# Deferring two thirds of the adaLN weights, and modulating a transposed x feature by feature

## What is computed

```python
def adaln(c, w_ada, b_ada):                      # c: 9 conditioning vectors (1 prompt, 8 samples)
    mod = jax.nn.silu(c) @ w_ada + b_ada         # w_ada is 1024 x 6144
    return mod.reshape(c.shape[0], 6, 1, D_MODEL)

def rmsnorm(x, g):
    xf = x.astype(jnp.float32)
    y = xf * lax.rsqrt(jnp.mean(jnp.square(xf), axis=-1, keepdims=True) + RMS_EPS)
    return (y * g.astype(jnp.float32)).astype(x.dtype)

def modulate(x, g, shift, scale):
    return rmsnorm(x, g) * (1.0 + scale) + shift

# modulate(x, g_mix, mod[:, 0], mod[:, 1]) is multiplied by w_in (1024 x 2856). Everything else
# (GLA, sparse attention, w_out, mixture of experts) comes after; mod[:, 2:6] is used only from w_out on.
```

## Time and profile before

| | |
|---|---|
| time, median of 3 executions | 2257.75 us (2255.24 to 2261.09) |
| the profiled execution | 2257.95 us, its span 2256.0 us |
| the stage `project` | 0 to 313.76 us of the span |
| PE, DVE, ACT, POOL busy over the span | 1863.9, 1465.3, 1085.5, 401.4 us |

### The profile page before, as it was taken

The page is one execution under the profiler, slowest core; times in us unless marked ns, Lnnn a source line. Parts: engine busy times, 40 slices in busy tenths (PEclk is TensorE's granted clock), DMA queues, the critical chain, the costliest instruction groups (busy, mean ns, idle before and its releaser), DMA issues. The chain is left out here.

```text
span 2256.0 us, 26455 instructions
## 1 busy us (share of the span) xinstructions
PE 1863.9 (83%) x8759; PEld 1403.3 (62%) x8759; DVE 1465.3 (65%) x1326; ACT 1085.5 (48%) x1015; POOL 401.4 (18%) x289
## 2 busy tenths in 40 slices
PE   7559976678886557707999999999999999999981
PEld 0038855466665343405777878787877778787861
DVE  1062227724443324436899898989898998989883
ACT  4021122333331111314767777777767677777761
POOL 0000010021000214040222222322222222223110
PEclk9769987696987678958999999999999999999996
DMA  4822142223000326046999999999999999999973
GB/s 177 346 93 70 39 89 101 62 89 113 1 1 3 111 98 188 24 124 242 351 357 377 361 369 368 370 368 361 377 354 380 360 377 361 375 366 370 372 269 106
DMA packets 119979, 525.52 MB, mean 233 GB/s; under 512 B 33629, under 2 KB 55022, under 8 KB 69327
## 3 DMA queue, kind: packets, MB, share of 16 engines
q1 hardware_dynamic: 105824, 487.26, 57.3%
q0 software_dynamic: 14096, 37.51, 6.7%
HBM read 503.17 MB, written 33.00 MB: 238 GB/s over the span
## 5 line engine op out<-in xcount | busy, mean ns | idle before, releaser
L2014 PE MATMUL banks<-split 128*128 128x512 f32 x4608 | 1086.8, 394 | 20.0 <-DVE split L2159 20.0
L2014 PEld LDWEIGHTS banks<-split 128*128 128x128 f32 x4608 | 858.7, 189 | 224.9 <-DVE split L2159 42.0
L2159 DVE TENSOR_TENSOR split<-expert_buffers,split 128x2048 fp32r<-128x2048 f32 x384 | 856.6, 2286 | 104.0 <-ACT split L2092 104.0
L2092 ACT ACTIVATE split<-expert_buffers 128x2048 fp32r<-128x2048 f32 x384 | 724.0, 1911 | 194.5 <-PE banks L2014 148.1
L1954 POOL TENSOR_TENSOR expert_buffers<-expert_buffers 128x1 f32<-128x1 f32 x64 | 66.8, 1044 | 775.8 <-issue 422.4
L2021 PE MATMUL banks<-expert_buffers 128*128 128x128 f32 x512 | 68.3, 277 | 58.7 <-DMA expert_buffers<-h_rows,expert_buffers 58.7
L1973 POOL DMA_INDIRECT ffn_rows<-expert_buffers x32 | 108.5, 3392 | 5.1 <-issue 4.6
L2021 PEld LDWEIGHTS banks<-expert_buffers 128*128 128x128 f32 x512 | 67.8, 192 | 63.8 <-issue 58.7
L408 PE MATMUL banks<-w_in_high,hT_high 128*128 128x476 f32 (+1 forms) x240 | 92.0, 383 | 1.5 <-ACT hT_high L278 1.5
L2107 ACT ACTIVATE expert_buffers<-expert_buffers 128x1024 f32<-128x1024 f32 x32 | 33.9, 1060 | 122.7 <-DVE expert_buffers L2170 122.7
L408 PE MATMUL banks<-w_in_low,hT_high 128*128 128x476 f32 (+1 forms) x240 | 91.7, 382 | 0.0
(11 more groups left out here) (310 smaller groups left out, 1924.4 us busy)
## 6 DMA issues: line engine op xcount, KB each, us to landing
expert_buffers<-in_w_gate SPq DMA_DIRECT2D x128, 1024.0 KB, 5.8
expert_buffers<-in_w_up SPq DMA_DIRECT2D x128, 1024.0 KB, 7.7
expert_buffers<-in_w_down SPq DMA_DIRECT2D x128, 1024.0 KB, 10.8
arena<-in_w_ada SPq DMA_DIRECT2D x8, 3072.0 KB, 12.3
w_in_landing<-in_w_in SPq DMA_DIRECT2D x6, 1904.0 KB, 8.5
arena<-in_x_prompt SPq DMA_DIRECT2D x8, 512.0 KB, 18.4
arena<-in_cache_cmp POOLq DMA_DIRECT2D x32, 128.0 KB, 3.3
arena<-in_cache_cmp SPq DMA_DIRECT2D x32, 128.0 KB, 2.8
```

What stands on the lines that cost most here:

```text
L2014: last = pe.matmul(ps[:, bank + c, :], x[:, kt * P:(kt + 1) * P].bitcast(F32R), wt.bitcast(F32R), start=False, stop=(kt == KT - 1 and x is ...
L2092: act.activation(high[:, j % RING_Q].bitcast(F32R), v, ACT.Copy).then_inc(s_high, 1)
L2159: dve.tensor_tensor(rest[:, j % RING_Q].bitcast(F32R), v, high[:, j % RING_Q], ALU.subtract).then_inc(s_rest, 1)
```

## The change

x is loaded ahead of any of w_ada. Of w_ada only the columns of shift and scale (the first 2048 of 6144) are loaded at first, in four pieces of 2 MB with buffers of their own; the other 4096 columns follow as 16 pieces of 1 MB, in two buffers that lie over x, and PE handles each after a given step of the projection (`place_of`), from step 5 to step 27 of 30. The first three chunks of w_in have buffers of their own and are queued right behind. The bias is loaded into `mod` beforehand and DVE adds the matmuls' result to it; the second part of that is done after the last step, and then columns 2048 to 6143 of `mod` are stored.

x, scaled only by its reciprocal root mean square, is transposed while w_ada arrives. Shift and scale are turned into columns by matmuls of 9 rows with the identity (L380's spreading is gone), and the modulation acts on the transposed x: `full(kt)` on a block of 128 features and all tokens, then ACT's rounding and DVE's rest for that block. The first four steps of the projection run block by block over four tiles at once; each block waits for its own rest.

```diff
@@ sp @@
+            sp.dma_start(c9[0:1, :], io["c_prompt"]).then_inc(s_c, 16)
+            sp.dma_start(c9[1:9, :], io["c_sample"]).then_inc(s_c, 16)
+            sp.dma_start(core.consts, io["consts"][:, 0:N_CONST_A + N_CONST_B]).then_inc(s_const, 16)
+            for t, (t0, n) in enumerate(TILES):
+                src = io["x_prompt"][0, t0:t0 + n, :] if t < ST else io["x_sample"].rearrange("b t d -> (b t) d")
+                sp.dma_start(x[0:n, t, :], src).then_inc(s_x, 16)
+            for i in range(4):
+                sp.dma_start(early[i], w_ada[:, 2 * i:2 * i + 2, 0:2 * D]).then_inc(s_early[i], 16)
             for j in range(4):
+                sp.dma_start(mod[32 * j:32 * j + 9, :, :], io["b_ada"].rearrange("a (b j n) -> a b j n", b=3, j=4)[:, :, j, :]
+                             .to_broadcast([9, 3, 512])).then_inc(s_b, 16)
+            sp.dma_start(gT, io["g_mix"].rearrange("a (p k) -> (a p) k", k=KT)).then_inc(s_g, 16)
+            for c in range(3):
+                load_w_in(c)
+            load_late(0)
+            load_late(1)
+            for i in range(NT, STEPS):
+                if i % NT == 0 and i // NT + 2 < NCH:
+                    load_w_in(i // NT + 2)
+                if i in place_of and place_of[i] + 2 < LATE:
+                    load_late(place_of[i] + 2)
+            sp.wait_ge(s_modcp, 12)
+            for j in range(4):
+                sp.dma_start(core.mod_d.rearrange("s (b j n) -> s b j n", b=3, j=4)[:, 1:3, j, :],
+                             mod[32 * j:32 * j + 9, 1:3, :]).then_inc(s_modout, 16)
             sp.wait_ge(s_modout, 64)
@@ act @@
+            for t, (t0, n) in enumerate(TILES):
+                link(act.activation(junk[0:n, :], x[0:n, t, :], ACT.Square, accum_out=stat[0:n, t:t + 1]))
             act.wait_ge(s_const, 16)
+            link(act.activation(stat[:, NT:2 * NT], stat[:, 0:NT], ACT.Ln, scale=1.0 / D, bias=core.const("eps")))
+            act.activation(stat[:, NT:2 * NT], stat[:, NT:2 * NT], ACT.Exp, scale=-0.5).then_inc(s_rstd, 1)
+            for t, (t0, n) in enumerate(TILES):
+                act.wait_ge(s_xT, t + 1)
+                act.activation(hT[:, 0:4, t0:t0 + n], x_banks(t)[:, 0], ACT.Copy).then_inc(s_xTa, 1)
             act.wait_ge(s_mod, 1)
             round_weights(0)
+            for kt in range(KT):
+                act.wait_ge(s_full, kt + 1)
+                act.activation(hTh[:, kt, :].bitcast(F32R), hT[:, kt, :], ACT.Copy).then_inc(s_hh, 1)
@@ dve @@
+                dve.tensor_scalar(tmp[0:n, t % 2, :], x[0:n, t, :], stat[0:n, NT + t:NT + t + 1], None, ALU.mult
+                                  ).then_inc(s_xn, 1)
+                if t >= 1:
+                    columns(t - 1)
...
+            dve.wait_ge(s_b, 64)
+            take_mod(0, 1)
+            dve.wait_ge(s_modT, 1)
...
+            def full(kt):
+                s = hT[:, kt, SEQ:NTOK].rearrange("p (b t) -> p b t", t=TS)
+                dve.tensor_scalar(hT[:, kt, 0:SEQ], hT[:, kt, 0:SEQ], scaleT[:, kt, 0:1], shiftT[:, kt, 0:1], ALU.mult, ALU.add)
+                link(dve.tensor_tensor(s, s, bcast(scaleT[:, kt, 1:9], 2, TS), ALU.mult))
+                dve.tensor_tensor(s, s, bcast(shiftT[:, kt, 1:9], 2, TS), ALU.add).then_inc(s_full, 1)
+            def rest_of_rows(kt):
+                dve.wait_ge(s_hh, kt + 1)
+                dve.tensor_tensor(hTl[:, kt, :].bitcast(F32R), hT[:, kt, :], hTh[:, kt, :], ALU.subtract).then_inc(s_hl, 1)
+            full(0)
+            rest_of_weights(0)
+            for kt in range(KT):
+                if kt + 1 < KT:
+                    full(kt + 1)
+                rest_of_rows(kt)
             rest_of_weights(1)
...
+            dve.wait_ge(s_mod, 2)
+            for b in (1, 2):
+                for j in range(4):
+                    rows = slice(32 * j, 32 * j + 9)
+                    dve.tensor_tensor(mod[rows, b, :], mod[rows, b, :], ps[rows, ADA + b, :], ALU.add).then_inc(s_modcp, 1)
@@ pe @@
+            for kt in range(KT):
+                if kt % 2 == 0:
+                    pe.wait_ge(s_early[kt // 2], 16)
+                last = modulation(kt, 0, early[kt // 2][:, kt % 2, :])
+            last.then_inc(s_mod, 1)
+            for n in range(4):
+                pe.wait_ge(s_modcp, n + 1)
+                rows = slice(32 * n, 32 * n + 9)
+                mv = mod[rows, 0, :].rearrange("s (p k) -> s k p", k=KT)
                 for kt in range(KT):
+                    last = pe.matmul(ps[64 * (n % 2):64 * (n % 2) + 64, XT + n, kt * 9:kt * 9 + 9], mv[:, kt, :],
+                                     ident[rows, 32 * n:32 * n + 9], start=True, stop=True)
+            pe.wait_ge(s_wl, 1)
+            for kt in range(KT):
+                pe.wait_ge(s_hl, kt + 1)
+                for t in range(ST):
+                    last = product(0, t, kt)
+                    if kt == KT - 1:
+                        last.then_inc(s_pj, 1)
+            for i in range(ST, STEPS):
...
+                if i in place_of:
+                    q = place_of[i]
+                    pe.wait_ge(s_late[q % 2], 16 * (q // 2 + 1))
+                    last = modulation(q // 2, 1 + q % 2, late[q % 2])
+                    last.then_inc(s_lateused if q < LATE - 1 else s_mod, 1)
```

More of the change, by code:

```diff
@@ L178, in project @@
                           for name, at, n in (("w_in_landing", 0, 3), ("w_in_low", 0, 3), ("w_in_high", 3, 2)))
-    ring = own.take(5 * CH)
+    own.take(3 * CH)
+    early = [core.arena[:, own.at + i * 4 * D:own.at + (i + 1) * 4 * D].rearrange("p (k n) -> p k n", k=2) for i in range(4)]
+    own.take(2 * CH)
     hTh, hTl = (core.named(name, own.at + i * KT * NTOK, KT * NTOK).rearrange("p (k n) -> p k n", k=KT)
@@ L292, in _ @@
             link = linker(dve, s_dve)
+            dve.memset(stat, 1.0).then_inc(s_one, 1)
             dve.wait_ge(s_cexp, 1)
@@ L344, in _ @@
+            def rest_of_rows(kt):
[7 more added lines that the diff above has]
+                rest_of_rows(kt)
             rest_of_weights(1)
-            for i in range(NCH * NT):
+            for i in range(STEPS):
                 c, t = divmod(i, NT)
@@ L362, in _, with modulation @@
+            def modulation(kt, b, piece):
+                for j in range(4):
+                    last = pe.matmul(ps[32 * j:32 * j + 9, ADA + b, :], scT[:, kt, :], piece[:, j * 512:(j + 1) * 512],
+                                     start=(kt == 0), stop=(kt == KT - 1))
+                return last
             pe.wait_ge(s_scT, 1)
-            pe.wait_ge(s_b, 16)
             for kt in range(KT):
-                pe.wait_ge(s_ada[kt % 2], 16 * (kt // 2 + 1))
-                for n in range(12):
-                    b, j = divmod(n, 4)
-                    out = ps[32 * j:32 * j + 9, 1 + b, :]
-                    if kt == 0:
-                        pe.matmul(out, core.const("exp_p")[0:1, 0:9], brow[:, n * 512:(n + 1) * 512], start=True, stop=False)
-                    last = pe.matmul(out, scT[:, kt, :], piece[kt % 2][:, n * 512:(n + 1) * 512],
-                                     start=False, stop=(kt == KT - 1))
-                last.then_inc(s_adaused if kt < KT - 1 else s_mod, 1)
@@ new lines, in _, with terms, product @@
+            last.then_inc(s_modT, 1)
+            pe.wait_ge(s_scaled, 4)
+            def terms(c):
+                return ((hTh, whigh[c % 2]), (hTh, wlow[c % 3]), (hTl, whigh[c % 2]))
+            def product(c, t, kt):
+                t0, n = TILES[t]
+                for j, (h, w) in enumerate(terms(c)):
+                    last = pe.matmul(ps[0:n, 4 + (NT * c + t) % 4, 0:CW], h[:, kt, t0:t0 + n].bitcast(F32R),
+                                     w[:, kt, :].bitcast(F32R), start=(kt == 0 and j == 0),
+                                     stop=(kt == KT - 1 and j == 2))
+                return last
@@ L405, in _ @@
                 for kt in range(KT):
-                    terms = [(hTh, whigh[c % 2]), (hTh, wlow[c % 3]), (hTl, whigh[c % 2])]
-                    for j, (h, w) in enumerate(terms):
-                        last = pe.matmul(ps[0:n, 4 + i % 4, 0:CW], h[:, kt, t0:t0 + n].bitcast(F32R),
-                                         w[:, kt, :].bitcast(F32R), start=(kt == 0 and j == 0),
-                                         stop=(kt == KT - 1 and j == 2))
-                last.then_inc(s_pj, 1)
+                    last = product(c, t, kt)
```

181 lines of the change are left out of this document (70 added, 111 removed).

## The result

The changed kernel takes 2182.34 us (median; 2175.89 to 2184.29) against 2256.49 us before; the ratio is 0.9651 (95% interval 0.9619 to 0.9684). The profiled execution took 2184.29 us, with a span of 2182.6. On another chip the changed kernel took 2181.57 against 2265.37, ratio 0.9632 (0.9607 to 0.9656). The forecast was 2187, in a range of 2172 to 2210.

The account below looks back on a forecast made before the run. The first stage was taken as bounded by a chain until 153.98 us, then by PE. Start -97.9, projection +17.0 and tail +10.3 gave -70.6 us, so 2187 us, range 2172 to 2210.

Parts of the forecast that it names:

- (a) to (d): Start of first stage: silu(c) by 15 to 16 us, x landed 12.9, root mean squares 22.0, transposes done 31.5.
- (e): Modulation of shift and scale on PE, 64 instructions, ending at 40.5 us, between 38.4 and 45.1.
- (f): Turning shift and scale into columns: 64 small PE instructions in 7.0 us (3.5 to 16.6), step ending at 49.2.
- (g): DVE's work up to the projection's first block: 6.9 us with waits, so PE starts at 56.1.
- The projection: First stage's projection: 16 late modulation calls on PE, 0.86 us each plus 0.2, lengthen it by 17.0 us.
- The tail: End of first stage: eight DVE additions and four stores after the last copy add 10.3 us (9 to 13).
- Sum: First stage's start, projection and tail together: -97.9 + 17.0 + 10.3 = -70.6 us.
- D: Projection: narrow calls bring the clock back to 1.2 GHz; 2317 us, slower by 60; 3 in 100.
- C: Projection: each of 14 later pieces arrives some 4 us too late; 2243 us; 3 in 100.
- E: Projection's first blocks wait for each other, 4.8 in place of 2.6 us a block, +18; 2205 us; 3 in 100.
- A: Small work before the projection is dearer, PE starts at 65 to 71; 2204 us (2198 to 2215); 12 in 100.
- B: Whole start quicker, clock up from transposes, small matmuls halved, PE starts at 50; 2177 to 2181 us; 12 in 100.

Follow-up runs that it names:

- e1: Kernel before with only the bias taken from PE, loaded into mod and added by DVE, the 12 bias matmuls gone: 2227.54 us, ratio 0.9845.
- e4: Changed kernel with the transposes of x put behind the modulation of shift and scale on PE: 2189.41 us, ratio 0.9695.
- e2: Changed kernel with every late call of four modulation matmuls made twice, the second time into a spare bank: 2197.33 us, ratio 0.9731.
- e3: Changed kernel with the last eight additions to mod, and the stores behind them, made inside the projection after the last late call: 2170.68 us, ratio 0.9604.
- e12: Changed kernel with one buffer for the late pieces in place of two: 2183.01 us, ratio 0.9648.
- e5: Changed kernel with the projection's first four steps tile by tile, PE waiting for all eight blocks: 2196.67 us, ratio 0.9700.
- e7: Changed kernel with DVE's rest of w_in's first chunk cut in four, each quarter made just before its blocks: 2182.95 us, ratio 0.9643.
- e8: Changed kernel with the edits of e3 and e7 together: 2172.21 us, ratio 0.9600.
- e11: Changed kernel with the edits of e3 and e7 and nine idle matmuls in PE's remaining wait before the projection: 2168.01 us, ratio 0.9563.

## Why the prediction was right, step by step

- **A stage that ends at a barrier** carries its gain one to one: 73.6 us in the stage, 73.4 in the span.
- **What bounded the kernel before.** That the first piece's matmuls with the bias take until 58.2 was read rightly, and e1 shows that 30 us hang on them. The reason given, the shared group of columns, is not shown (e1). No term of the sum rests on it.
- **(a) to (d), rows and statistics.** x at 13.6 (forecast 12.9), the root mean squares at 22.6 (22.0), the transposes done at 31.0 (31.5). scT was out at 14.2, earlier than I let it be (15 to 16), since SP asks for c first now; it was not the last there either.
- **(e) Modulation.** 37.95 in place of 40.5: the one step of the start whose size was off. I took a value between a clock that rises 2.5 us before the end of the stretch and one that is up from its start; the transposes had raised it, and the 16 sets of four instructions ran at 0.44 us each (7.05). e4 confirms it from the other side.
- **(f) Small matmuls.** 6.46 us for 64, 0.1 each from start to start, against 7.0; L360 was the right row of the two bounds (3.5 and 16.6 us), but not for its clock: the granted clock fell from 1.00 to 0.50 in this window, and the distance stayed. The four DVE instructions took 1.1, against 1.0.
- **(g) DVE's work ahead of the first block.** 6.6 us (46.48 to 53.12) against 6.9. The start fell at 53.1, not 56.1; 2.5 of these 3 us are step (e). w_in's first chunk was late by my count (41.7 in place of 39) and hidden all the same.
- **The projection.** +18.4 against +17.0: beyond its matmuls a call costs 0.3 us where I allowed 0.2 (e2). Nothing waited for a late piece.
- **The tail.** +8.9 against +10.3. The additions took 5.7 us (forecast 5.2), but the four stores were issued in 1.38 us, where the row before had 3.42 and I had 2.6 up to the last. e3 shows that the mechanism was the one named. From the last issue's end (237.4) to the next stage it is 2.8 us. The fixed cost of about 2.0 us in the Trainium skill (DMA: Bandwidth & Descriptors, "Anatomy of one DMA") is given there for transfers that GpSimd issues, and these come from SP; it would fit inside the 2.8 us, but no row shows the landing of a store apart.
- **Sum.** -100.9 + 18.4 + 8.9 = -73.6, against -97.9 + 17.0 + 10.3 = -70.6. The measured median is 4.7 us below the forecast: 3 from the sum, 2 because the profiled execution was itself 2 us above the median. That the sum is off by only as much as the start is luck: the projection is 1.4 us dearer than its term and the tail 1.4 cheaper.
- **The rivals.** D, the narrow calls taking the clock away, is refuted by the window at 1.00 and by e2, which doubled them; in e4 narrow matmuls alone brought a burst to the full pace. C, late pieces on the chain, is refuted even with one buffer (e12), and by more than I had argued: I had counted 4 us in hand at the tightest place. E is refuted by PE's windows, busy without a gap from 53.12 on, and by e5: the block-by-block order wins 9 us. A did not come: PE started 12 us before its earliest time. B was right in that the clock was up from the transposes on, and wrong for the small matmuls, whose distance stayed 0.1 us.
- **What the prediction did not ask**: how much of the gain the bias matmuls alone were. 30 us of it could have been had with e1's few lines.

## What to carry to other kernels

Look at which of an early phase's results its successor needs, and put the rest under the first stretch that another engine bounds: the price is that work in full on the bound engine (here 0.86 us a call and 0.3 on top), the gain is the whole wait. Moved work brings its own ending with it; put the final additions and stores where an engine still has something to run beside them, not behind the last step. And before a long first burst is accepted, look at the distance of its matmuls: with a one-row bias matmul in turn they came 1.8 us apart, 3.6 us a pair and 43 us for twelve pairs, where twelve bare ones took 4.5 us (e1).

## What the runs showed of the hardware

- At the head of a trace the granted clock in the record need not fit the pace. In e4 it stands at 1.00 for the first three bursts of one form, of which the first two took 3.60 us for 16 instructions and the third 1.91. In the kernel before it is 1.00 from 18 to 58 us, with instructions 0.9 us apart. There it should be checked against the distance of instructions.
- The projection's instructions went from 0.40 to 0.22 us apart 3.7 to 6.1 us after the start of the projection in the runs without idle matmuls (3.7 in e5 and e7, 4.4 in e2, 5.6 in the changed kernel twice, 6.1 in e3 and e8).
- Matmuls of 9 stationary rows, 64 stationary columns and 9 moving ones followed each other at 0.1 us, while the granted clock went from 1.00 (38 to 40 us) to 0.50 (42 to 45.4); loading the stationary side took 0.21 us each.
- The stages between the first and the loading of w_out (the attention among them) took 517.9 us in the kernel before, 519.0 and 518.6 in the two profiles of the changed one, 514.4 in e2, 521.1 in e11, 524.4 in e7 and 528.2 in e3, without an edit in them. PE was busy for 359 us of them in e2 and for 372 in e3, at a mean granted clock of 0.78 and 0.76:

```profile
252.70:767.10 514.40, 359.07 (x2107) 271.37 (x2107) 234.46 (x542) 145.77 (x380) 55.75 (x93) 0.78 0.22 63
```

```profile
231.32:759.50 528.18, 372.21 (x2107) 281.46 (x2107) 234.57 (x542) 146.15 (x380) 55.77 (x94) 0.76 0.22 61
```

The whole times of one kernel spread as much: six executions of e3 lie 16.3 us apart. Whether these 14 us are such a spread, or whether an edit in the first stage shifts them, the traces do not say, since the two profiles of one kernel agree to 0.4 us. That the clock in the short bursts of these stages has a part in it is a guess; no run separates it. For an edit of under 5 us in the first stage, the end of the stage is a better measure than the whole time, good to the 1 or 2 us by which PE's start and the rise of the clock differ between runs.
